# Loading each weight half of a two-layer decoder step in two transfers with a signal each

## The reference, cut to what matters

```python
def layer(x, p, C, n, m, buf, start, ...):
    h = rmsnorm(x, norm1)
    proj = h @ w_in                            # 1024 x 2568: q, k, v, o, pooling, gates
    ... mLSTM heads, causal pooling ...
    mix = jnp.concatenate([hm, zp], axis=-1).astype(x.dtype) @ w_out      # 1024 x 1024
    x = x + mix
    x = x + peer_ffn(rmsnorm(x, norm2), peer_wq, peer_keys, peer_u, peer_v)
    x = x + jax.nn.sigmoid(x @ w_gate) * (p.astype(x.dtype) @ w_ple)
    return x, C_new, n_new, m_new, buf_new

def block_fn(xb):                              # in peer_ffn
    q = (xb @ wq)...                           # 1024 x 2048
    s = jnp.einsum('thcd,chkd->thck', q, keys)
    ... top 16 of 128 twice, then top 16 of the pairs: eidx, gate ...
    ue = u_tab[eidx]
    act = jax.nn.gelu(jnp.einsum('td,thkd->thk', xb, ue).astype(jnp.float32))
    ve = v_tab[eidx]
    return jnp.einsum('thk,thkd->td', (gate * act).astype(xb.dtype), ve)
```

## Time and profile before

| what | value |
|---|---|
| median of 3 runs | 1671.47 us (1671.4 to 1674.97) |
| profiled execution: its time | 1673.4 us |
| profiled execution: its span, first to last instruction | 1671.2 us |
| instructions | 19424 |
| bytes moved | 682.03 MB, mean 408 GB/s |
| mean granted TensorE clock | 0.857 of full speed |
| weight loads | 102 of 1024 KB |
| gathers | 256 + 256 + 16 |

### The profile page before, as it was taken

One profiled execution on the slowest core, in us unless ns is written; L12 is line 12 of the kernel. 1 busy time (PEld: TensorE's weight loads), 2 busy tenths in 40 slices (PEclk: granted clock), 3 DMA queues, 4 the chain that ended last, 5 costly groups with the idle time before them and its releaser, 6 DMA issues. The chain is left out here.

```text
span 1671.2 us, 19424 instructions
## 1 busy us (share of the span) xinstructions
PE 1311.7 (78%) x6310; PEld 495.1 (30%) x6310; DVE 1013.2 (61%) x2625; ACT 704.7 (42%) x1976; POOL 499.7 (30%) x532
## 2 busy tenths in 40 slices
PE   8978896788967798876676898668985776676677
PEld 4534343334412333321112344223441221111113
DVE  1468566846986336797555443855799654455454
ACT  3245554434344444334333464433343453333334
POOL 0032323322232123234333223323234333333330
PEclk9987998899988999997657999789997886676669
DMA  8699999999999999999999999999999999999994
GB/s 336 252 400 426 372 425 422 422 419 426 425 394 408 426 426 414 427 425 427 427 428 426 426 408 425 423 424 411 421 426 426 426 426 427 427 427 427 427 427 169
DMA packets 96018, 682.03 MB, mean 408 GB/s; under 512 B 11024, under 2 KB 12560, under 8 KB 14238
## 3 DMA queue, kind: packets, MB, share of 16 engines
q0 software_dynamic: 76032, 553.68, 79.1%
q1 hardware_dynamic: 19886, 127.12, 18.6%
HBM read 674.63 MB, written 6.59 MB: 408 GB/s over the span
## 5 line engine op out<-in xcount | busy, mean ns | idle before, releaser
L2172 DVE SCALAR_TENSOR_TENSOR rows<-rows,shown 128x1024 f32<-128x1024 f32 x528 | 637.5, 1220 | 499.2 <-DMA rows<-in_uv,index_B 270.0
L1294 PE MATMUL acc<-rows,weighted 128*64 128x512 f32 x2048 | 661.1, 753 | 213.9 <-ACT weighted L1697 208.6
L1503 POOL DMA_INDIRECT rows<-in_uv,index_A x256 | 242.9, 949 | 638.8 <-PE acc L1294 487.0
L981 PE MATMUL bank<-wring,turned 128*128 128x512 f32 (+1 forms) x832 | 384.7, 610 | 10.1 <-DMA wring<-in_w 8.1
L1503 POOL DMA_INDIRECT rows<-in_uv,index_B x256 | 241.6, 944 | 469.8 <-PE acc L1294 438.0
L1294 PEld LDWEIGHTS acc<-rows,weighted 128*64 128x64 f32 x2048 | 135.6, 158 | 644.4 <-ACT weighted L1697 490.5
L981 PEld LDWEIGHTS bank<-wring,turned 128*128 128x128 f32 x832 | 156.9, 197 | 195.4 <-issue 183.0
L1686 ACT ACTIVATE dots_B<-dots_B 128x1 f32<-128x1 f32 x256 | 51.8, 202 | 369.2 <-DVE rows L2172 360.2
L1686 ACT ACTIVATE dots_A<-dots_A 128x1 f32<-128x1 f32 x256 | 51.5, 201 | 318.6 <-DVE rows L2172 312.7
L1697 ACT ACTIVATE weighted<-consts,dots_A 128x64 f32<-128x64 f32 x256 | 89.0, 348 | 8.4
L1697 ACT ACTIVATE weighted<-consts,dots_B 128x64 f32<-128x64 f32 x256 | 89.0, 348 | 8.4
(11 more groups left out here) (315 smaller groups left out, 960.2 us busy)
## 6 DMA issues: line engine op xcount, KB each, us to landing
wring<-in_w SPq DMA_DIRECT2D x102, 1024.0 KB
out_sample<-scratch SPq DMA_DIRECT2D x2, 2128.5 KB
scratch<-in_c_s SPq DMA_DIRECT2D x2, 2064.0 KB, 15.8
rows<-in_uv,index_A POOLq DMA_INDIRECT x256
rows<-in_uv,index_B POOLq DMA_INDIRECT x256
keys<-in_keys SPq DMA_DIRECT2D x2, 1024.0 KB, 14.3
gain<-in_gain SPq DMA_DIRECT2D x3, 640.0 KB, 8.4
consts<-in_consts SPq DMA_DIRECT2D x1, 1243.0 KB, 10.9
```

The lines of the kernel that those rows point to most:

```text
L981: ins = pe.matmul(ps[:, part], turned["A"][:, 4 * h + c, :], w[:, c, part], start=first, stop=end, skip_group_check=True)
L1294: ins = pe.matmul(acc[c * 64:(c + 1) * 64, :], weighted[:, n % STATS, :], row[:, c * BLOCK:(c + 1) * BLOCK], start=first, stop=end, skip_g ...
L1503: pool.indirect_dma_start(out=rows[:, n % RING, :], out_offset=None, in_=a["uv"], in_offset=bass.IndirectOffsetOnAxis(ap=index[kind][:, pa ...
L2172: dve.scalar_tensor_tensor(u, u, 1.0, shown[:, :, :], ALU.mult, ALU.mult, accum_out=dots[kind][:, part, i:i + 1]).then_inc(u_used, 1)
```

## The change

Each of the 102 ring halves is loaded by two transfers, blocks 0 and 1 and then blocks 2 and 3, 512 KB each: 128 partitions of 4 KB out of the same 8 KB lines. Each has a semaphore of its own for each ring slot. `half` waits for the first as before; `half_rest` waits for the second, in `dense` ahead of block 2, in `embed` right at its start. The half APART stays one transfer. When SP may issue is unchanged.

```diff
+        half_rest_in = [sem(f"half_rest_in{i}") for i in range(WRING)]
...
+            def half_rest(e):
+
+                if e != APART:
+                    n = HALF_OF[e]
+                    pe.wait_ge(half_rest_in[n % WRING], 16 * (n // WRING + 1))
...
                 for c in range(4):
+                    if c == 2:
+                        half_rest(half_key((name, p, j, h)))
...
             def embed(p):
                 w = half(half_key(("embed", p)))
+                half_rest(half_key(("embed", p)))
...
-                sp.dma_start(wring[:, n % WRING].rearrange("p c n -> p (c n)"),
-                             a["w"][layer, half_index(e)]).then_inc(half_in[n % WRING], 16)
+                for landed, c0 in ((half_in, 0), (half_rest_in, 2)):
+                    sp.dma_start(wring[:, n % WRING, c0:c0 + 2].rearrange("p c n -> p (c n)"),
+                                 a["w"][layer, half_index(e), :, c0 * BLOCK:(c0 + 2) * BLOCK]).then_inc(landed[n % WRING], 16)
```

## The result

The changed kernel takes 1679.7 us (median of 8 runs, 1678.39 to 1682.07); the kernel before has a median of 1672.65 us in its 8 runs. The ratio is 1.0042, 95% interval 1.0028 to 1.0055: slower by some 7 us. 3.7 us slower were forecast; the interval of the ratio is 4.7 to 9.2 us, so the forecast shift was too small, while the stated range of 1669.5 to 1683 holds the median.

What follows compares the result with a forecast made beforehand. PE was taken to bound the start, the DMA engines some 1550 us after it. Packets +4.2 us and start -0.5 us gave +3.7 us on 1671.5, so 1675.2 us, range 1669.5 to 1683.

Steps and rivals of the forecast that it cites:

- The prediction's own signs of being wrong: First gather moves over 1 us, DMA share falls below 1.0 in full stretches, or gaps sum to other than 7 us.
- its three places: Where DMA engines run dry: 165 to 175, 470 to 515 and 970 to 980 us, together 7.0 us.
- the rival of opened gaps: Late halves widen gaps where DMA runs dry, named at the second prompt tile's index: 1680.2 us, chance 0.16.
- What bounds the kernel: PE and its dependency chains set the start, DMA engines some 1550 us after it, then a tail.
- Part 1: 82 loads from 90 us on, where DMA is full: 9 more packets per engine at 5.7 ns, +4.2 us.
- Part 2: First half: its first piece lands 1.2 us sooner, PE starts at about 7.05 instead of 7.57 us, -0.5 us.
- Part 3: 102 more transfers issued by SP and a second PE wait in every half: 0 us.
- Part 4: Beside gathers, queues alternate by packet: first blocks 1.2 us sooner, last two 2.5 us later; price 0 unless gaps open.
- the likeliest case: Packets cost 4 to 9 ns, gaps stay as now within 1 us: 1673 to 1678 us, chance 0.60.
- Gaps close: Gathers run ahead beside weights and all 7.0 us of gaps close: -4.5 us, 1667.0 us, chance 0.10.
- Starts hidden: Engines hide packets' starts: 0 to 3 us added less 0.5, 1671.0 to 1674.0 us, chance 0.12.
- A cost of each transfer's own: Each transfer pays an unhidden time, 0.45 us for each of 82: 37 us, 1708 us, chance 0.02.

Runs made afterwards that it cites:

- The cut at the first gather: Two kernels against the kernel before: only the 20 halves loaded before the first gather in two transfers, 1.0006; only the 82 from number 20 on, 1.0047.
- The 8 KB cut: Against the kernel before, each half in two transfers by even and odd partitions, 8 KB packets, PE waiting for both in front of block 0: 1.0005.
- the burst whole: The changed kernel, but halves 49 to 58, loaded back to back between 536 and 605 us, in one transfer each: 1.0024 against the kernel before.

## Why the prediction was right, and where not

**The prediction's own signs of being wrong.** It named three, and said that then latency and not packets decided. The first gather moved by 1.2 us, over the 1 us allowed. The share, full there before, was 0.75 from 575 to 590 us. The gaps were not the 7 us of its three places any more. So latency did have a part, though packets kept theirs: the one transfer with 4 KB lines and the two with 8 KB lines show that. The forecast shift was half of the measured one; the range held the result because it had room for the rival of opened gaps, not because the sum had the gap.

**What bounds the kernel: right.** The cut at the first gather (1.0006 and 1.0047) shows that the price is paid in the DMA-full stretches.

**Part 1, packets: right in kind, probably a quarter to a third too small.** The forecast was 4.2 us; the profiles show 5.6 us, 7.5 ns for each (6.2 us by the stretches of 20 us), and the transfer in one piece with 4 KB lines 5.5 us recorded, 3.6 after the overlap. The 8 KB cut, with 1.0005, excludes the number of transfers alone as the cause; with 4 KB lines, two transfers cost 0.36% more than one where PE waits for the whole half, and the sum had no term for that. The term was mis-sized by its unit price: two packets of 4 KB recorded alone are 9 ns more than one of 8 KB, while inside the stream the recorded price was 8 to 10 ns with one transfer, 10 to 11 with two and 12 with four of 2 KB. Why it is higher with more pieces no run here shows.

The Trainium skill (Trace Analysis, section DMA Optimizations) says that splitting may complete the overall task sooner if the DMA engines are generally idle. The trace agrees with the condition as far as it goes: here the engines were full (share 1.01) and the split kernel was slower, 1.0042. The other side, a gain on idle engines, no run here shows.

**Part 2, start: wrong.** Forecast -0.5 us, the profiled execution had +1.2; by the means of three and four profiles it is +0.7. The step that failed is the landing of the first piece, "1.2 us at 427 GB/s" sooner. Stretch from 4.5 to 9 us, before and after:

```profile
4.50:9.00 4.50, 3.40 (x10) 2.41 (x11) 1.70 (x4) 2.73 (x4) 0.00 (x0) 1.00 1.02 421
```

```profile
4.50:9.00 4.50, 2.85 (x9) 2.07 (x10) 1.70 (x4) 2.73 (x4) 0.00 (x0) 1.00 0.95 303
```

With the hardware queue alone at work, it moved 303 GB/s and not 421. The smaller lines explain little of that. The same stretch with 4 KB lines in one transfer, and with 8 KB lines in two (even and odd partitions):

```profile
4.50:9.00 4.50, 2.64 (x9) 2.07 (x10) 1.70 (x4) 2.73 (x4) 0.00 (x0) 1.00 1.03 405
```

```profile
4.50:9.00 4.50, 1.97 (x8) 1.57 (x8) 1.70 (x4) 2.73 (x4) 0.00 (x0) 1.00 0.88 331
```

The rate falls mostly where there is a second transfer. It repeats: 421, 416 and 426 GB/s in the profiles with whole halves, 280 to 303 in the five with two transfers of 4 KB lines. The small transfers behind them are late next: with the burst whole, PE began at 7.03 us as forecast and then waited for `m_s`:

```profile
7.03 5.93 PE L994 MATMUL bank<-wring,turned 128*128 128x512 f32 x8 [0.15 <-DMA wring<-in_w]
13.93 1.95 PE L1035 MATMUL bank<-w_gates,turned 128*128 128x8 f32 x16 [0.98 <-DMA m_s<-in_m_s]
```

I had let them leave 0.45 us later and priced that at 0; in the changed kernel SP issues `m_s` at 5.75 us instead of 4.04, since two more issues stand ahead of it and its issues took longer. What is open: why a second transfer lowers the rate, and why one transfer with 4 KB lines, at 405 GB/s, still let PE begin only at 8.33 us (two with both waits began at 9.98 with 4 KB lines and at 9.14 with 8 KB). Whether the late start reached the end at all the timings can't say: starts late by 1.3 and 2.3 us came with ratios of 1.0006 and 1.0005, whose intervals hold both 0 and the full amount.

**Part 3, instructions of SP and PE: right in the full stretches,** by the cut into even and odd partitions; at the start SP's issues count, as said.

**Part 4, turns by packet: right; its price of 0 wrong.** The two queues sent 230 and 227 packets, and their shares of 67.8% and 34.3% are the 309 to 159 ns that the step used, and the place it named, the burst from 531 us, is where it struck. What failed is "all that while the DMA engines work". They work while PE waits, but they work off all that is queued, and when PE at last has its half, both queues are empty until it has used it: 3.9 us. The term belonged in the sum. PE's wait for this half grew by 3.5 us, to 10.7.

**The rivals.** Gaps open: it happened beside the likeliest case, at another place than the one it named; from 470 to 530 us the gap closed instead. Gaps close: there, at 165 and at the end, 4.1 us in all (2.9 if the end is moved by 9.9 us), while 6.0 opened. Starts hidden: out, by the recorded packets and by the 1.0037 with one transfer. A cost of each transfer's own: out at its price of 0.45 us (37 us in all) and not seen with 8 KB lines, but with 4 KB lines two transfers took some 6 us more than one.

**Only argued: the smaller gap at 1370 to 1385 us,** 2.1 of the 6.0. The waits of the kernel after from 1360 to 1390 us look like the burst's:

```profile
POOL rows L1514 <- PE acc L1303: 20.9, 4, 15.7
...
PEld bank L990 <- DMA wring<-in_w: 4.2, 2, 2.6
```

PE waits for weights, where the kernel before has no such wait from 1350 to 1381 us, and GpSimd's longest wait for PE is 15.7 us instead of 7.8. But with only the first 20 halves in two PE also waited for weights, up to 3.5 us, between 1350 and 1360 us, and that kernel had no gap. And this gap doesn't come with every run of the same loads: with the halves from number 20 on in two, PE had the very same waits for `wring` there (4.2 us, two, the longest 2.6) and the share was 0.99, and with only the burst whole it was 1.01. So it may be one of the gaps that come and go from run to run; no run here took this place alone.

## What to carry to other kernels

In a kernel that keeps its DMA engines full, price a finer cut of transfers by the packets it adds, and expect more than the recorded time of single packets says (here 9 ns by that, some 10 in the stream). If transfers must be smaller, keep the lines whole and give each transfer alternate partitions; never a contiguous half of them, which cost 20% here. Where two queues send equal numbers of packets whatever their size, shrinking the packets of one also gives its bandwidth to the other: look for the place where several of its loads stand back to back, and ask what is still queued at the moment the starved engine resumes. And count how often a kernel's gaps differ between profiles of like kernels before one of them is explained: here the share from 165 to 185 us was 0.86 and 0.96 in two profiles of the same kernel.

## What the runs showed of the hardware

Cut by partitions 0 to 63 and 64 to 127, the same 8 KB packets took far longer, and the kernel 20% longer. Its hardware queue from 200 to 400 us:

```profile
q1 hardware_dynamic: 2071, 13.37, 24.1%
```

24.1% of 16 x 200 us = 771 us for 13.37 MB, 1632 packets of 8 KB: 0.47 us each, where the kernel before has 0.31 us. Even and odd partitions, just as many for each transfer, show nothing of it (15.5%, as before). Both cuts give a transfer 64 partitions, so it matters which partitions it writes, not how many. The other surprise is the one above: alone at work at the start, the hardware queue carried 421 GB/s with 8 KB lines and 405 with 4 KB lines in one transfer, but 303 and 331 (4 and 8 KB) where each half came in two transfers; beside gathers two transfers of 4 KB lines hardly lowered the rate, 420 instead of 422.
